# Decay arguments of the state space groups: made by TensorE and ScalarE from on-chip rows instead of loaded by DMA

## The chip, the cores and the metric

The kernel runs on one core of one Trainium2 chip. The metric is the device time of one execution in microseconds (us), as the median of some runs. All times below are for that one core.

## The reference, cut to what matters

The kernel computes two transformer-like blocks over 512 tokens of width 1024. The change touches the first block's state space branch: 32 heads in 8 groups of 4 (R = 4), each run forwards and backwards over 4 chunks of 128 tokens.

```
xbc = silu(depthwise_conv(xbc, conv_w, conv_b))        # 5 taps
a_cs   = cumsum(dt * a)                                # per head, within a chunk
decay  = exp(where(mask, a_cs[l] - a_cs[s], -inf))     # 128 x 128 per head, chunk, direction
cb     = einsum('bclgn,bcsgn->bcgls', c, b)
y_diag = einsum('bcgls,bcgrls,bcsgrp->bclgrp', cb, decay, xdt)
states = einsum('bclgn,bcgrl,bclgrp->bcgrpn', b, decay_states, xdt)
y_off  = einsum('bclgn,bcgrpn,bcgrl->bclgrp', c, prev, exp(a_cs))
y = y_diag + y_off + xs * d_skip;  y = y * silu(z)     # then a norm per group
```

The argument of the decay is the difference of two entries of the same cumulative sum. For each head one of them runs along the 512 tokens in a row, the other is a number per partition.

## The kernel before, in words

**Weights.** All large matrix products stream their weights. SyncE loads `raw` in quarters (`load_quarter`, L240), ScalarE rounds it to `w_hi` (`make_hi`, L248), GpSimd makes the remainder `w_lo` (`make_lo`, L255), and TensorE runs three products for each (`main_step`, L279). One step is 12 matmuls of 512 columns; a panel is 8 steps. A `w_hi` can be written only when the step that used that place, a panel earlier, is done.

**A group.** Under 12 such steps TensorE does a group's small products (`ssd_pe`, L1550): states after step 2 (two) and step 4 (one), the four heads' `pe_y` after steps 3, 4, 5 and 6, the products with the earlier states `pe_off` 0 after step 6 and 1 and 2 after step 7, and for the next group the transposes and the c by b product `pe_turn` (0, 1 after step 9; 2, 3 after step 11). Four PSUM banks `main` hold the panels. Four more, `aux0` to `aux3`, hold the small products: `aux0` and `aux1` the result y of all four heads, `aux2` and `aux3` everything else in turn. The semaphores `aux_free` say how often `aux2` and `aux3` have been emptied. `pe_off(2)` writes `aux3`, so it waits for VectorE to have emptied `pe_off(0)` from it (`take_off(0)`).

**Decay.** `cs_dram` holds the rows of the cumulative sum. ScalarE's queue loads for each head both directions' rows, spread over all partitions, into `dmat[r]` (`load_decay`, L582: 512 KB). VectorE subtracts the per-partition number twice (L1800), takes the smaller of both directions into `e_buf` (L1801), ScalarE exponentiates (L1232), and VectorE multiplies with `cb_m` (`weigh`, L1805).

**VectorE's order in a group** (`ssd_group`, L1790): `xdt` (L1846), decay 0 and 1, weigh 0 and 1, decay 2 and 3, states 0 and 1 (L1813 to L1819), weigh 2 and 3, states 2, first pair of the next group's convolution (L1760 the centre tap, L1769 the four others), `take_off` 0 to 2 (L1830, L1840), second pair of the convolution, y from `aux0` and `aux1` (L1869), the gate (L1872), `mask_cb` (L1779). GpSimd does `xw` (L1079, two of 1024 columns) and the skip term (L1083) at a group's start and otherwise `w_lo`. ScalarE does `w_hi`, the Silus (L1193), the copies out of the banks (`take_x`, L1187, twice per pair of groups; `take_turned`, L1198 and L1202), and the squares (L1274). The order on each engine is written out by hand; seven cycles lead from group 0 to group 7, and groups 0 to 5 run in a loop of pairs (`half` 0 and 1).

**Before group 0**, ScalarE's queue also stores 4 MB of attention bias rows (`rel_rows`, L1180).

Of the kernel before, what the change touches and what calls it, by code (L numbers as in the profile page):

```python
# [24 lines left out]
P = 128  # L25
# [66 lines left out]
def two_blocks(nc, d, out):  # L92
    ctx = ExitStack()
    with ctx:
# [44 lines left out]
        cst_sb = at("cst_sb", B0 + 60 * KB, [64, TOK])  # L139
# [19 lines left out]
        e_buf = [at("e_buf0", R0 + 32 * KB, [P, TOK]), at("e_buf1", R0 + 34 * KB, [P, TOK])]  # L159
# [65 lines left out]
        cs_dram = nc.dram_tensor("cs_rows", (2, G, R, TOK), F32, kind="Internal").ap()  # L225
# [117 lines left out]
        cs_stored, rel_stored = sem("cs_stored"), sem("rel_stored")  # L343
# [228 lines left out]
        decay_landed = [sem(f"decay_landed{h}") for h in range(R)]  # L572
        xdt_done, xw_done, skip_done = sem("xdt_done"), sem("xw_done"), sem("skip_done")
        arg_done, decay_done, t_done = sem("arg_done"), sem("decay_done"), sem("t_done")
        states_full = sem("states_full")
# [5 lines left out]

        def load_decay(eng, g, r):  # L582

            if isinstance(g, int):
                src = bass.AP(cs_dram.tensor, (g * R + r) * TOK, [[0, P], [NH * TOK, 2], [1, TOK]])
            else:
                row = cs_dram[:, bass.ds(g, 1), r, :]
                src = bass.AP(row.tensor, row.offset, [[0, P], [NH * TOK, 2], [1, TOK]])
            eng.dma_start(dmat[r][:, :, :], src).then_inc(decay_landed[r], 16)

# [19 lines left out]
        def pe_turn(eng, g, part):  # L610
# [14 lines left out]
        def pe_states(eng, g, i):  # L625
# [8 lines left out]
        def pe_y(eng, g, r):  # L634
# [8 lines left out]
        def pe_off(eng, g, i):  # L643
# [485 lines left out]
        def _(act):  # L1129
# [47 lines left out]
            act.wait_ge(dt_dve, 4)  # L1177
            act.dma_start(cs_dram.rearrange("a g r t -> (a g r) t"), cst_sb[:, :]).then_inc(cs_stored, 16)
# [5 lines left out]
            def take_x(p):  # L1184
                for m in range(4):
                    wait_full(act, p, p, m)
                    act.activation(u_raw[:, m, :], mb[m][:, :], ACT.Copy).then_inc(bank_free, 1)  # L1187

# [23 lines left out]
            take_turned(0, 0)  # L1212
            hi(2, range(6, 7))
# [3 lines left out]
            hi(2, [7])  # L1217

            def ssd_act(gp, half):
# [10 lines left out]
                def decay_exp(r):  # L1230
                    act.wait_ge(arg_done, g * 4 + r + 1)
                    act.activation(e_buf[r % 2][:, :], e_buf[r % 2][:, :], ACT.Exp).then_inc(decay_done, 1)  # L1232

                decay_exp(0)
                decay_exp(1)
                slots(0, 4 - half)
# [6 lines left out]
                decay_exp(2)  # L1243
                decay_exp(3)
                slots(4, 7)
                if not last:
                    for r in range(R):
                        act.wait_ge(y_full, g * 4 + (r + 1))
                        load_decay(act, g + 1, r)
# [5 lines left out]
                if not last:  # L1255
# [3 lines left out]
                    slots(8, 9)  # L1259
# [23 lines left out]

# [177 lines left out]
        def _(pe):  # L1461
# [74 lines left out]
            def turn_first(k):  # L1536
# [7 lines left out]
                if k == 5:  # L1544
                    pe_turn(pe, 0, 2)
                if k == 6:
                    pe_turn(pe, 0, 3)
# [631 lines left out]
```

## Time and profile before

| | us |
|---|---|
| median of 3 runs | 2009.14 (2003.4, 2009.14, 2009.41) |
| the profiled execution | 2006.3 |
| its span | 2004.5 |
| first `xdt` of group 0 | 103.79 |
| first `xdt` of group 7 | 515.85 |

The profile is one execution of the program. Its span is 1.8 us shorter than that execution's time. Times in its rows count from the span's start. Durations of neighbouring VectorE, ScalarE and TensorE rows overlap by some hundredths to tenths of a microsecond, since one instruction drains while the next starts; the pace is the distance of the starts.

### The profile page before, as it was taken

To read this page: it belongs to the slowest core of one execution; us is meant where nothing else is said; L and a number is where in the kernel's file an instruction comes from. 1 tells how busy PE (TensorE), PEld (TensorE's weight loads), DVE (VectorE), ACT (ScalarE), POOL (GpSimd) and SP (SyncE) were. 2 spreads that over 40 slices of the span, in tenths; PEclk is the share of its full clock that TensorE was granted. 3 is DMA by queue.
4 is the path that set the end of the run, shared out by engine and by line. 5 is a ranking of instruction groups with operands and counts; after the bars stand their busy time and mean duration, and the time that the engine had idled before them with its cause. 6 is when DMAs were issued, how large, how long until landed. Compare 5 with 4: busy or idle time off the path is not lost.

```text
span 2004.5 us, 27105 instructions
## 1 busy us (share of the span) xinstructions
PE 1838.4 (92%) x8948; PEld 1518.2 (76%) x8948; DVE 964.1 (48%) x1306; ACT 793.2 (40%) x1627; POOL 841.3 (42%) x598
## 2 busy tenths in 40 slices
PE   5698898898789999998999999999989999999988
PEld 4577677777668787877888888877878888787766
DVE  4389898999931456423432022132072112445754
ACT  4233333334232465532443234334343332466542
POOL 4244443445734312243554444454474444441312
PEclk9898998999889999999999999999999999999989
DMA  4742223233112312142323333333323223221111
GB/s 156 138 139 63 91 84 105 94 94 88 60 45 93 111 43 89 47 132 74 94 90 100 95 95 95 102 97 126 94 74 95 84 84 99 80 79 52 63 32 53
DMA packets 55011, 176.76 MB, mean 88 GB/s; under 512 B 5291, under 2 KB 7723, under 8 KB 54668
## 3 DMA queue, kind: packets, MB, share of 16 engines
q1 hardware_dynamic: 38592, 140.53, 22.9%
q10 hardware_dynamic: 16332, 35.11, 6.5%
q8 instruction: 50, 0.82, 0.2%
q14 instruction: 37, 0.30, 0.1%
HBM read 169.19 MB, written 6.42 MB: 88 GB/s over the span
## 4 chain that ended last, share of the span: by engine, by line
PE 62%; DVE 18%; issue 12%; POOL 4%; ACT 3%; DMA 1%; DVEq 1%; ACTq 0%; POOLq 0%
PE main L294 46%; DVE dmat L1800 5%; PE aux L773 3%; PE main L322 3%; POOL w_lo L257 2%; PE main L1604 2%; DMA dmat<-cs_rows 1%; PE aux L638 1%; DVE y_all L1840 1%; PE aux L760 1%; PE aux L747 1%; DVE u_acc L1769 1%; PE aux L364 1%; DVE dmat L1805 1%; DVE off_t L1830 1%
## 5 line engine op out<-in xcount | busy, mean ns | idle before, releaser
L257 POOL TENSOR_TENSOR w_lo<-raw,w_hi 128x512 fp32r<-128x512 f32 x504 | 709.0, 1414 | 1035.9 <-ACT w_hi L253 1021.9
L253 ACT ACTIVATE w_hi<-raw 128x512 fp32r<-128x512 f32 x486 | 301.7, 629 | 697.3 <-PE main L294 684.2
L294 PE MATMUL main<-w_hi,a_hi 128*128 128x512 f32 x752 | 319.1, 424 | 2.3 <-ACT vv L1381 1.4
L294 PE MATMUL main<-w_hi,a_lo 128*128 128x512 f32 x752 | 299.7, 399 | 0.0
L294 PE MATMUL main<-w_lo,a_hi 128*128 128x512 f32 x752 | 299.3, 398 | 0.0
L294 PE MATMUL main<-a_hi,w_hi 128*128 128x512 f32 x576 | 235.9, 410 | 2.2 <-ACT u_raw L1187 2.2
L294 PE MATMUL main<-a_lo,w_hi 128*128 128x512 f32 x576 | 228.5, 397 | 0.0
L294 PE MATMUL main<-a_hi,w_lo 128*128 128x512 f32 x576 | 228.2, 396 | 0.0
L294 PEld LDWEIGHTS main<-w_hi,a_lo 128*128 128x128 f32 x752 | 144.6, 192 | 32.2
L294 PEld LDWEIGHTS main<-w_hi,a_hi 128*128 128x128 f32 x752 | 145.9, 194 | 30.3 <-ACT vv L1381 1.8
L294 PEld LDWEIGHTS main<-w_lo,a_hi 128*128 128x128 f32 x752 | 146.0, 194 | 24.5
L294 PE MATMUL main<-w_hi,f_hi 128*128 128x512 f32 x352 | 139.3, 396 | 1.6 <-DVE f_lo L377 1.6
L294 PE MATMUL main<-w_hi,f_lo 128*128 128x512 f32 x352 | 137.8, 391 | 0.0
L294 PE MATMUL main<-w_lo,f_hi 128*128 128x512 f32 x352 | 137.7, 391 | 0.0
L294 PEld LDWEIGHTS main<-a_hi,w_hi 128*128 128x128 f32 x576 | 111.4, 193 | 26.0 <-issue 3.1
L294 PEld LDWEIGHTS main<-a_hi,w_lo 128*128 128x128 f32 x576 | 110.8, 192 | 24.0
L294 PEld LDWEIGHTS main<-a_lo,w_hi 128*128 128x128 f32 x576 | 111.4, 193 | 22.8
L773 PEld LDWEIGHTS aux<-v_sb,pt 128*128 128x128 f32 x544 | 70.3, 190 | 40.6 <-ACT pt L844 23.2
L1769 DVE SCALAR_TENSOR_TENSOR u_acc<-u_raw,par,u_acc 128x510 f32<-128x510 f32 (+1 forms) x128 | 97.1, 828 | 0.0
L1800 DVE TENSOR_TENSOR dmat<-dmat,cs_sb 128x512 f32<-128x512 f32 x64 | 91.4, 1428 | 4.1 <-DMA dmat<-cs_rows 0.5
L773 PE MATMUL aux<-v_sb,pt 128*128 x544 | 83.6, 279 | 6.2 <-ACT pt L844 3.9
L814 ACT ACTIVATE pr<-lg,small 128x384 f32<-128x384 f32 (+1 forms) x128 | 70.5, 553 | 24.8 <-DVE small L800 24.8
(287 smaller groups left out, 3098.5 us busy)
## 6 DMA issues: line engine op xcount, KB each, us to landing
raw<-w_stream_in SPq DMA_DIRECT2D x264, 512.0 KB, 3.5
dmat<-cs_rows ACTq DMA_DIRECT2D x32, 512.0 KB, 9.4
x_res<-x_in ACTq DMA_DIRECT2D x8, 512.0 KB, 4.8
rel_rows<-rel_row ACTq DMA_DIRECT2D x1, 4096.0 KB, 44.4
bias<-rel_rows ACTq DMA_DIRECT2D x2, 1536.0 KB, 7.7
out<-x_res SPq DMA_DIRECT2D x4, 512.0 KB, 2.6
bgate<-b_gate_in ACTq DMA_DIRECT2D x4, 256.0 KB, 5.5
ln_g<-ln_g_in ACTq DMA_DIRECT2D x1, 1024.0 KB, 6.6
```

The lines of the kernel that those rows point to most:

```text
L253: eng.activation(w_hi[:, k, :], raw[:, k, :], ACT.Copy).then_inc(hi_done, 1)
L257: eng.tensor_tensor(w_lo[:, k, :], raw[:, k, :], w_hi[:, k, :].bitcast(F32), ALU.subtract).then_inc(lo_done, 1)
L294: mm = eng.matmul(mb[m][:, :], lhs, rhs, start=(first and k == 0 and n == 0), stop=(last and k == KT - 1 and n == 2))
L322: mm = eng.matmul(out, lhs, rhs, start=(first and k == 0 and n == 0), stop=(last and k == KT - 1 and n == 2))
L364: t = eng.transpose(b[:, m * P:m * P + P], self.src[:, m, c:c + P], ident)
L638: x = eng.matmul(ab[c // 2][:, (c % 2) * GW + r * HP:(c % 2) * GW + r * HP + HP], dmat[r][:, dr, c * P:c * P + P], xdt[:, dr, c, r * HP:r ...
L747: eng.matmul(ab[c % 2][:, 0:nb * P], q, self.k_hh[half][:, keys], start=True, stop=False)
L773: x = eng.matmul(ab[3][:, c * HP:c * HP + HP], pt[c % 2][:, b * P:b * P + P], v_sb[:, lo + b, bass.ds(j * P + half * HP, HP)], start=(b == ...
L814: eng.activation(pr[t % 2][:, c, 0:self.w], lg[t % 2][:, c, 0:self.w], ACT.Exp, bias=small[:, ng + c:ng + c + 1], accum_out=small[:, sm + ...
L1604: mm = pe.matmul(mb[m][:, :], lhs, rhs, start=False, stop=(k == KT - 1 and n == 2))
L1769: ins = dve.scalar_tensor_tensor(acc, u_raw[:, m, i0:i0 + o1_ - o0], tap(m, k), acc, ALU.mult, ALU.add)
L1800: ch(dve.tensor_tensor(dm[:, dr], dm[:, dr], cs, ALU.subtract))
```

## The change

Nothing is loaded for the decay any more. The rows of the cumulative sum stay on chip, rounded part in the upper and remainder in the lower 64 partitions of `cs_hl`; `pick` and `picked` hold ones that choose a head's two rows.

- TensorE: `pe_arg` (two matmuls of 512 columns per head) writes a head's row, spread over all partitions, to `aux0` (one direction) and `aux1` (the other). Head 0 runs after step 8 and waits for `y_taken` (VectorE has taken the last group's y from both banks); heads 1, 2 and 3 run after steps 9, 10 and 11, each behind `arg_done` of the head before.
- ScalarE: `take_arg` copies `aux0` with the per-partition number added, in four pieces of 128 columns, into the head's own half tile `dmat[r][:, 1]`. The exponential works there in place. `centre` does the convolution's centre tap and bias (four instructions per group). Four DMA issues per group go.
- VectorE: `arg_min` adds the number to `aux1` and takes the minimum with the tile, in four pieces of 128 columns. The 8 subtractions of L1800, 4 minima of L1801 and 4 centre taps of L1760 per group go.
- Order on VectorE: states 2 stands behind the convolution's first pair, y is taken right after the second pair, and all of `take_off` comes behind y. Weigh 0, 1 and 2 stand ahead of the states.

```diff
-        def load_decay(eng, g, r):
...
+        def pe_arg(eng, g, r, half):
+
+            if r == 0:
+                eng.wait_ge(pick_set, g + 1)
+                if not (isinstance(g, int) and g == 0):
+                    eng.wait_ge(y_taken, g)
+            else:
+                eng.wait_ge(arg_done, g * 4 + r)
+            for dr in range(2):
+                one_row = picked[:, half, dr, r:r + 1].broadcast_to((P, P))
+                x = eng.matmul(ab[dr][:, :], one_row, cs_hl[:, :], start=True, stop=True)
+            x.then_inc(arg_full, 1)
...
+            def centre(g, taken, pair):
...
+                    act.activation(u_acc[:, m, :], u_raw[:, m, :], ACT.Identity, bias=par[:, bass.ds(g * 4 + (PC["conv_b"] + m), 1)],
+                                   scale=par[:, bass.ds(g * 20 + (PC["conv_w"] + m * 5 + 2), 1)]).then_inc(centred, 1)
+
+            def take_arg(g, r):
+
+                act.wait_ge(arg_full, g * 4 + (r + 1))
+                if not (isinstance(g, int) and g == 0):
+                    act.wait_ge(y_full, g * 4 + (r - 3))
+                for c in range(NT):
+                    cs = slice(c * P, c * P + P)
+                    x = act.activation(dmat[r][:, 1, cs], ab[0][:, cs], ACT.Identity, bias=cs_sb[:, c, bass.ds(g * R + r, 1)])
+                x.then_inc(arg_in, 1)
...
             take_x(0)
+            act.wait_ge(dt_dve, 4)
+            pick_rows(0, 0)
+            centre(0, 0, 0)
+            centre(0, 0, 1)
             hi(2, range(0, 3))
-            for n in range(4):
-                silu(0, n)
-            hi(2, range(3, 6))
-            act.wait_ge(cs_stored, 16)
-            for r in range(R):
-                load_decay(act, 0, r)
+            act.wait_ge(dt_dve, 6)
+            take_arg(0, 0)
+            silu(0, 0)
+            silu(0, 1)
...
                     silu(g + 1, 2)
                     silu(g + 1, 3)
+                    slots(8, 9)
+                    take_arg(g + 1, 0)
                     slots(9, 10)
                     take_turned(g + 1, 0)
+                    take_arg(g + 1, 1)
                     slots(10, 11)
                     if half == 1:
                         take_x(gp * 3 + (P_Z + 2))
+                    take_arg(g + 1, 2)
+                    decay_exp(g + 1, 0)
                     slots(11, 12)
                     take_turned(g + 1, 2)
                     take_turned(g + 1, 3)
+                    take_arg(g + 1, 3)
+                    decay_exp(g + 1, 1)
+                    decay_exp(g + 1, 2)
...
+            def arg_min(g, r):
+
+                dve.wait_ge(arg_in, g * 4 + (r + 1))
+                for c in range(NT):
+                    e = dmat[r][:, 1, c * P:c * P + P]
+                    x = dve.scalar_tensor_tensor(e, ab[1][:, c * P:c * P + P], cs_sb[:, c, bass.ds(g * R + (NH + r), 1)], e,
+                                                 ALU.add, ALU.min)
+                x.then_inc(arg_done, 1)
+
             conv(0, 0, 0)
+            arg_min(0, 0)
             conv(0, 0, 1)
+            arg_min(0, 1)
             mask_cb(0)
+            arg_min(0, 2)
...
-                decay(0)
-                decay(1)
+                arg_min(g, 3)
                 weigh(0)
                 weigh(1)
-                decay(2)
-                decay(3)
+                weigh(2)
                 take_states(0)
                 take_states(1)
-                weigh(2)
                 weigh(3)
-                take_states(2)
                 if not last:
                     conv(g + 1, gp * 12 + (4, 12)[half], 0)
-                for i in range(3):
-                    take_off(i)
+                take_states(2)
                 if not last:
                     conv(g + 1, gp * 12 + (4, 12)[half], 1)
...
+                dve.wait_ge(y_taken, g + 1)
+                for i in range(3):
+                    take_off(i)
+                if not last:
+                    arg_min(g + 1, 0)
```

What stands in a row on VectorE behind the convolution's first pair of group 1, before (`off_t<-aux3` is `take_off(0)`, which frees `aux3`):

```order
L1769 ISA [waits dve_chain]
L1769 SCALAR_TENSOR_TENSOR u_acc_98<-u_raw_97,par_56,u_acc_98 128x510
L1830 REGISTER_ALU [waits off_full]
L1830 TENSOR_TENSOR off_t_101<-aux3,e_cs_59 128x256
L72 REGISTER_ALU
L1830 ISA [waits dve_chain]
```

And behind the second pair of the same group, in the changed kernel:

```order
L1827 SCALAR_TENSOR_TENSOR u_acc_100<-u_raw_99,par_56,u_acc_100 128x510
L1926 ISA [waits skip_done,y_full]
L1926 TENSOR_TENSOR y_all_85<-y_all_85,aux0 128x2x256
L72 REGISTER_ALU
L1926 ISA [waits dve_chain]
L1926 TENSOR_TENSOR y_all_85<-y_all_85,aux1 128x2x256
L1891 REGISTER_ALU [waits off_full,y_taken]
L1891 TENSOR_TENSOR off_t_101<-aux3,e_cs_59 128x256
L72 REGISTER_ALU
L1891 ISA [waits dve_chain]
L1891 TENSOR_TENSOR off_t_101<-aux3,e_cs_59 128x256
```

`take_off(0)` has moved from between the two pairs to behind both of them and behind the two additions of y.

On TensorE, the small products after step 7 of group 0 in the changed kernel (as before, the third waits for `aux3`):

```order
L658 MATMUL aux2<-hst_97,c_st_88 128x256 [waits aux2_free]
L658 MATMUL aux2<-hst_97,c_st_88 128x256
L658 MATMUL aux3<-hst_97,c_st_88 128x256 [waits aux3_free]
L658 MATMUL aux3<-hst_97,c_st_88 128x256
L282 REGISTER_ALU
```

And after step 9 of the same group, before:

```order
L622 MATMUL aux2<-const_55,u_acc_98 128x128 [waits silu_done]
L622 MATMUL aux2<-const_55,u_acc_98 128x128 x3
L615 REGISTER_ALU [waits aux3_free]
L620 MATMUL aux3<-c_st_86,u_acc_98 128x128 [waits silu_done]
L620 MATMUL aux3<-c_st_86,u_acc_98 128x128 x3
L282 REGISTER_ALU
```

and in the changed kernel, with the argument of head 1 behind them:

```order
L626 MATMUL aux2<-const_55,u_acc_100 128x128 [waits silu_done]
L626 MATMUL aux2<-const_55,u_acc_100 128x128 x3
L619 REGISTER_ALU [waits aux3_free]
L624 MATMUL aux3<-c_st_88,u_acc_100 128x128 [waits silu_done]
L624 MATMUL aux3<-c_st_88,u_acc_100 128x128 x3
L611 MATMUL aux0<-cs_hl_77,picked_79 128x512 [waits arg_done]
L611 MATMUL aux1<-cs_hl_77,picked_79 128x512
```

TensorE gains two matmuls of 512 columns there, and with them a wait for VectorE's minimum of the head before.

## Rows read from the trace of the kernel before

**Rows 1.** Windows by cycle: length, busy PE PEld DVE ACT POOL, PEclk, DMA, GB/s.
```profile
282.90:343.00 60.10, 53.65 (x256) 45.00 (x256) 52.38 (x61) 22.49 (x46) 26.20 (x15) 0.90 0.33 91
458.90:515.80 56.90, 51.26 (x254) 43.13 (x254) 54.70 (x61) 19.57 (x38) 26.38 (x15) 0.95 0.33 93
```

**Rows 2.** Timeline, TensorE, group 3: start, us, instruction, [idle before it <-releaser].
```profile
305.56 2.07 PE L631 MATMUL aux<-xw,b_tok 128*128 128x256 f32 x4 [3.48 <-DVE hst L1813]
339.82 1.11 PE L622 MATMUL aux<-const,u_acc 128*128 128x128 f32 x4 [2.63 <-DVE cb_m L1779]
```

**Rows 3.** Chain of waits in order of time, group 3: start, us, work.
```profile
307.63 4.62 PE main L294 x12
313.98 2.81 PE main L294 x12
316.79 1.73 PE aux L638 x16
318.52 0.92 PE aux L652 x4
```

**Rows 4.** Timeline of VectorE in group 3.
```profile
282.88 2.36 DVE L1846 TENSOR_TENSOR xdt<-x_tok,dt_sb 128x1024 f32<-128x1024 f32 x2 [2.08 <-ACT x_tok L1202]
319.72 0.98 DVE L1830 TENSOR_TENSOR off_t<-aux,e_cs 128x256 f32<-128x256 f32 x2
329.38 5.37 DVE L1769 SCALAR_TENSOR_TENSOR u_acc<-u_raw,par,u_acc 128x510 f32<-128x510 f32 x8
334.67 1.40 DVE L1869 TENSOR_TENSOR y_all<-y_all,aux 128x512 f32 x2
```

**Rows 5.** Groups by line, VectorE, 282.8 to 343.0: busy, mean ns, idle before.
```profile
L1800 DVE TENSOR_TENSOR dmat<-dmat,cs_sb 128x512 f32<-128x512 f32 x8 | 11.7, 1465 | 0.6
L1801 DVE TENSOR_TENSOR e_buf<-dmat 128x512 f32<-128x512 f32 x4 | 5.3, 1324 | 0.1
L1760 DVE TENSOR_SCALAR u_acc<-u_raw,par 128x512 f32<-128x512 f32 x4 | 2.7, 721 | 0.6 <-DVE hst L1819 0.4 <-DVE y_all L1840 0.3
```

**Rows 6.** Timeline of GpSimd in group 3.
```profile
284.28 5.03 POOL L1079 TENSOR_TENSOR xw<-xdt,e_st 128x1024 f32<-128x1024 f32 x2 [2.46 <-DVE xdt L1846]
295.60 7.19 POOL L257 TENSOR_TENSOR w_lo<-raw,w_hi 128x512 fp32r<-128x512 f32 x4 [3.98 <-ACT w_hi L253]
```

**Rows 7.** One line's instructions each, whole span: duration ns min/median/max.
```profile
L1817 DVE TENSOR_TENSOR hst<-hst,dec x16: 676/692/2375, 128.0 to 543.7; 128x512 f32<-128x512 f32 x16
...
L1819 DVE TENSOR_TENSOR hst<-hst,aux x16: 686/686/689, 128.7 to 546.1; 128x512 f32<-128x512 f32 x16
...
L1830 DVE TENSOR_TENSOR off_t<-aux,e_cs x48: 409/424/426, 142.0 to 556.1; 128x256 f32<-128x256 f32 x48
```

**Rows 8.** Timeline of ScalarE in group 3.
```profile
285.05 1.28 ACT L1232 ACT_TABLE_LOAD   x1
336.83 2.05 ACT L1187 ACTIVATE u_raw<-main 128x512 f32<-128x512 f32 x4
339.26 0.62 ACT L1202 ACTIVATE x_tok<-aux 128x512 f32<-128x512 f32 x1
```

**Rows 9.** Timeline before group 0: ScalarE's queue, TensorE, VectorE.
```profile
81.93 14.53 ACTq L589 DMA_DIRECT2D dmat<-cs_rows  x4
...
97.16 1.11 PE L622 MATMUL aux<-const,u_acc 128*128 128x128 f32 x4 [15.27 <-ACT b_tok L1198]
...
103.79 2.40 DVE L1846 TENSOR_TENSOR xdt<-x_tok,dt_sb 128x1024 f32<-128x1024 f32 x2 [23.20 <-ACT x_tok L1202]
```

**Rows 10.** Weight loads of SyncE, 40 to 130 us, issue to landing.
```profile
DMA to landing us min/median/max: 3.5/3.6/18.4
```

**Rows 11.** Timeline of the last group: VectorE, GpSimd.
```profile
515.85 2.36 DVE L1846 TENSOR_TENSOR xdt<-x_tok,dt_sb 128x1024 f32<-128x1024 f32 x2 [0.38 <-ACT x_tok L1202]
558.95 1.22 DVE L1872 TENSOR_TENSOR y_all<-y_all,sz 128x1024 f32<-128x1024 f32 x1
...
540.26 13.27 POOL L603 TENSOR_TENSOR y_all<-y_all,ssq 128x1024 f32<-128x1024 f32 x6
```

More of the change, by code:

```diff
@@ L606, in y_group, with pe_turn @@
             return y_all[:, :, bass.ds(g * GW, GW)]
-        def pe_turn(eng, g, part):
+        def pe_arg(eng, g, r, half):
[9 more added lines that the diff above has]
+            x.then_inc(arg_full, 1)
+        def pe_turn(eng, g, part, half):
             bank = part % 2
@@ L623, in pe_turn, with pe_states @@
             x.then_inc(turned, 1)
-        def pe_states(eng, g, i):
+        def pe_states(eng, g, i, half):
             if i == 0:
@@ L632, in pe_states, with pe_y @@
             x.then_inc(states_full, 1)
-        def pe_y(eng, g, r):
+        def pe_y(eng, g, r, half):
+            if r == 0:
+                eng.wait_ge(arg_done, g * 4 + 4)
             eng.wait_ge(t_done, g * 4 + r + 1)
@@ L641, in pe_y, with pe_off @@
             x.then_inc(y_full, 1)
-        def pe_off(eng, g, i):
+        def pe_off(eng, g, i, half):
             bank = (i + 1) % 2
@@ L1187, in take_x, with decay_exp, pick_rows @@
                     act.activation(u_raw[:, m, :], mb[m][:, :], ACT.Copy).then_inc(bank_free, 1)
+            def centre(g, taken, pair):
+                two = TILES[2 * pair:2 * pair + 2]
+                act.wait_ge(bank_free, taken + (max(two) + 1))
+                for m in two:
+                    act.activation(u_acc[:, m, :], u_raw[:, m, :], ACT.Identity, bias=par[:, bass.ds(g * 4 + (PC["conv_b"] + m), 1)],
[8 more added lines that the diff above has]
+                x.then_inc(arg_in, 1)
+            def decay_exp(g, r):
+                act.wait_ge(arg_done, g * 4 + (r + 1))
+                act.activation(dmat[r][:, 1, :], dmat[r][:, 1, :], ACT.Exp).then_inc(decay_done, 1)
+            def pick_rows(g, half):
+                act.activation(picked[:, half], pick[:, :].rearrange("p (a h) -> p a h", a=2)[:, :, bass.ds(g * R, R)], ACT.Copy).then_inc(pick_set, 1)
             def silu(g, n):
@@ L1217, in _ @@
             hi(2, [7])
+            take_arg(0, 3)
+            for r in range(3):
+                decay_exp(0, r)
             def ssd_act(gp, half):
@@ L1228, in slots @@
                         make_hi(act, gp * 3 + (P_Z + 1 + q // 8), q % 8)
[L1230 to L1236, printed above, removed]
+                slots(0, 1)
+                decay_exp(g, 3)
+                if not last:
+                    pick_rows(g + 1, 1 - half)
+                slots(1, 4 - half)
                 if half == 1:
@@ L1242, in ssd_act @@
                     slots(3, 4)
-                decay_exp(2)
-                decay_exp(3)
-                slots(4, 7)
+                taken = gp * 12 + (4, 12)[half]
                 if not last:
-                    for r in range(R):
-                        act.wait_ge(y_full, g * 4 + (r + 1))
-                        load_decay(act, g + 1, r)
+                    centre(g + 1, taken, 0)
+                slots(4, 5)
+                if not last:
+                    centre(g + 1, taken, 1)
+                slots(5, 7)
                 if half == 0:
@@ L1281, in _ @@
             ssd_act(3, 1)
+            act.wait_ge(rel_stored, 16)
             op_y.act(act, [0, 1])
@@ L1758, in conv @@
                 dve.wait_ge(bank_free, taken + (max(two) + 1))
-                for m in two:
-                    ch.count(dve.tensor_scalar(u_acc[:, m, :], u_raw[:, m, :], tap(m, 2), par[:, bass.ds(g * 4 + (PC["conv_b"] + m), 1)],
-                                               ALU.mult, ALU.add))
+                dve.wait_ge(centred, g * 4 + (2 * pair + 2))
                 for k in (0, 1, 3, 4):
@@ L1867, in ssd_group @@
                         dve.wait_ge(y_full, g * 4 + 4)
+                        dve.wait_ge(skip_done, g + 1)
                     y2 = y_group(g)[:, 2 * t2:2 * t2 + 2, :]
-                    ch(dve.tensor_tensor(y2, y2, ab[t2][:, :].rearrange("p (c n) -> p c n", c=2), ALU.add))
+                    ins = dve.tensor_tensor(y2, y2, ab[t2][:, :].rearrange("p (c n) -> p c n", c=2), ALU.add)
+                    if t2:
+                        ins.then_inc(y_taken, 1)
+                    else:
+                        ch(ins)
+                dve.wait_ge(y_taken, g + 1)
+                for i in range(3):
+                    take_off(i)
+                if not last:
+                    arg_min(g + 1, 0)
                 dve.wait_ge(bank_free, gp * 12 + (4 * O_Z + 4))
@@ L1873, in ssd_group @@
                 if not last:
+                    arg_min(g + 1, 1)
                     mask_cb(g + 1)
-            per = len(TILES) * 4 + 1 + 2 * R + 2 + 3 + 6 + 2
+                    arg_min(g + 1, 2)
+            per = len(TILES) * 3 + 1 + 2 + 3 + 6 + 1
             with dve.Fori(0, 3) as gp:
```

70 lines of the change are left out of this document (36 added, 34 removed).

## The prediction

> **What bounds the kernel now.** I read three views, in this order. First the windows by group: a cycle, from one group's `xdt` to the next's, takes 57 to 60 us, TensorE is busy for 51 to 54 of them and VectorE for 52 to 55 [rows 1]. From 103.79 [rows 9] to 515.85 [rows 11] seven cycles take 412.1 us, 58.9 each. Then TensorE's timeline of group 3: it idles twice, 3.48 us for VectorE's state copy and 2.63 us for `mask_cb` [rows 2], both times because VectorE is late. Then the chain: behind such an idle a step takes 4.62 us, an undisturbed one 2.81 [rows 3]; the granted clock of a cycle is 0.90 to 0.95 [rows 1], so of 60.1 us some 12, of 56.9 some 6 ran at 1.2 instead of 2.4 GHz: 6 and 3 us of work lost for two idles, 1.5 to 3 for each. So VectorE sets the pace, through TensorE's waits and the clock after them. Before group 0, TensorE idles 15.27 us while ScalarE's queue issues four decay loads behind the 4 MB store (14.53 us) [rows 9].
>
> **The change part by part.** I follow one cycle, with T the start of `xdt` and group 3 as the model.
>
> Removed from VectorE: 8 L1800 and 4 L1801, 11.7 + 5.3 = 17.0 us, and 4 L1760, 2.7 us [rows 5]. Twelve instructions of about 0.69 us (the L1817 median, [rows 7]) would be 8.3, so 8.7 of the 17.0 is waiting. It falls where GpSimd works: `xw` and four `w_lo` run side by side with them [rows 6]. That GpSimd work stays, and what now stands beside it is `weigh` and the convolution, which read two SBUF tiles as L1800 did. The rows split by operand: L1817 (two SBUF inputs) goes from 676 to 2375 ns, L1819 and L1830 (one input from PSUM) stay within 686 to 689 and 409 to 426 [rows 7]. So I carry all 8.7 over to the new neighbours; the lower bound is 0. The Trainium skill (SBUF — State Buffer, "Who interferes with whom") says the same as a lock: of a VectorE instruction with two SBUF inputs and a GpSimd one that reads SBUF, the second to start blocks for the other's whole length. By that rule none of the 8.7 is saved; without it all of it would be.
>
> Added to VectorE: 16 pieces of `arg_min` with one PSUM input. 256 columns take 0.42 us [rows 7], 512 about 0.69, so 128 about 0.29: 1.15 us per head, 4.6 per group, of which head 3's stands behind `xdt` and three heads' at the end. Bounds 0.8 (pace without overlap of drains) and 2.8 per head (as 512-column instructions). Centre taps, ScalarE: 4 of about 0.62 us (as `x_tok`, [rows 8]); ScalarE idles long at those places, its bound is the same from above, nothing from below, and I take 0.
>
> The point that decides: **`take_off(0)` moves behind both convolution pairs and y**, and `pe_off(2)`, on TensorE after step 7, waits for it to empty `aux3`. Queued behind `pe_off(2)` are steps 8 to 11 and all arguments and transposes of the next group. VectorE's time from T to the end of `take_off(0)`'s products: before, T to the end of the second pair is 329.38 + 5.37 - 282.88 = 51.9 [rows 4]. Minus 17.0; minus 329.38 - 319.72 = 9.7 (all of `take_off` and two L1760) [rows 4]; minus the other two L1760, 1.3: 23.9. Plus 1.15 for head 3, plus 8.7 carried over, plus 1.4 for y and 1.0 for the products [rows 4], plus 1.3 for one `w_lo` more beside the second pair (295.60: 7.19 for four, 1.8 each with VectorE beside it) [rows 6]: **37.4 us**. Bounds: 27.4 (nothing carried over, no extra `w_lo`) and 40.
>
> TensorE reaches `pe_off(2)` 8 x 2.81 + four `pe_y` of 1.73 + four small products of about 0.9 [rows 3] = 33.0 us after its step 0 starts, and that start lies 0.3 to 1.9 us ahead of T. So it idles about 5 to 6 us there, where it now idles 3.5 and 2.6 elsewhere. Cost in clock: 1.5 to 3 us per idle from above; I take 2.3 once.
>
> From there TensorE leads: `pe_off(2)` 0.92, four steps 11.2, three arguments 3 x 2 x 0.23 = 1.4 (a step's 2.81 / 12 per matmul) [rows 3], two small products 1.1 (one of them at low clock took 1.11 [rows 2]): 14.6 to the end of step 11. The arguments' hand-overs (ScalarE 0.8, VectorE 1.15) are hidden by a step of 2.81 as long as ScalarE is free. Then, in the first group of a pair: transposes 1.1, `x_tok` 0.62 [rows 8], signals 0.3: 2.0. In the second, ScalarE does `take_x` ahead of `take_arg(2)`: copies after step 11 0.7 (the last of four in 2.05), `take_arg(2)` 0.8, table load 1.28 and exponential 0.63, a `w_hi` 0.5, two `x_tok` 1.1, signals 0.3 [rows 8]: 5.3. So the cycles are 37.4 + 14.6 + 2.3 + 2.0 = 56.3 and 59.6 us. Seven: 4 x 56.3 + 3 x 59.6 = 404.0 against 412.1: **-8 us**. The decay's shorter chain is nearly eaten by the later `take_off(0)`.
>
> Start: the 15.27 idle goes. New there: `take_x` behind three more small instructions (about 1.7), VectorE's second pair behind head 0's argument (which waits for TensorE's step 3), TensorE's head 2 behind that pair, and head 3's argument behind `take_x(1)`: I take 6 of them on the path. Net **-9**, bounds 0 and -15.3. The 4 MB store stays; it is needed only by the attention.
>
> Last group: before, 515.85 to the gate's end 560.2, 44.3 us [rows 11]. The 17.0 are gone there too, but `take_off` comes last, and GpSimd's six norms (13.27 [rows 11]), which read SBUF, then run beside its additions and the gate. I take **-5**, bounds 0 and -12.
>
> Sum: 2006.3 - 8 - 9 - 5 = 1984. The profiled execution (2006.3) is 2.8 below the median of the runs (2009.1), so I put **1987**.
>
> **The rivals.**
> - A, the waiting goes with the instructions: VectorE needs 33 us or less to `take_off(0)`, TensorE no longer idles, and a cycle is TensorE's work: 60.1 - 3.5 - 2.6 - 6 = 48 plus four arguments 1.9, 50, and 53 in second groups. Seven: 359, -53; with start and end 1942. Against: [rows 7] and [rows 6]. Chance 0.1. Half way (34 to 36 us and a shorter low clock), about 1965: 0.15.
> - B, slower: the arguments' round trips. TensorE may not start the next head before ScalarE and VectorE have finished the last. After 5 to 6 us idle step 8 runs at 1.2 GHz; if VectorE, with `take_off`, the gate and `w_lo` beside it, is later than TensorE at heads 1, 2 and 3, TensorE idles again after each step and stays at 1.2 GHz for more of the 14.6 us. Half of it more at that level is 4 us a cycle, 28 in all: 2015. It decides from 4 us a cycle on. For: 2.6 us idle already brings the low level [rows 2, 3]; against: the slack per head is a whole step. Chance 0.15.
> - C, the start gives nothing: the 4 MB store holds back the weight loads (18.4 us to landing against 3.6 [rows 10]), and an earlier group 0 waits for weights instead: 1996. Chance 0.12.
> - The forecast itself, 1975 to 2003: 0.48.
>
> **How the numbers follow.** About 0.3%, 6 us, is what a measurement of this kernel can tell from no change. The forecast gives 0.43 faster and 0.05 same or slower; A 0.25 faster; C 0.06 faster, 0.05 same, 0.01 slower; B 0.14 slower, 0.01 same: faster 0.74, same 0.10, slower 0.16. The range takes in the half-way case and B at its price, and leaves out A in full: 1948 to 2017.
>
> **What would show it.** In the profile after: TensorE idle 5 to 6 us before the third small product after step 7, released by VectorE's `off_t`, in all groups; hardly any idle before the states or the transposes. `weigh` (1024 columns, as `xdt`, of which two take 2.36 [rows 4]) well above 1.2 us for the first two of a group. `arg_min` pieces within 0.25 to 0.35 us whatever GpSimd does. Second groups some 3 us longer than first ones. First `xdt` near 92, with weigh 0 near 98. If the idle before `pe_off(2)` is under 2 us, A holds; if the idles stand before the arguments, B. I would be wrong altogether if VectorE got to `take_off(0)` as late as 40 us after T.

## The result and the profile after

The changed kernel takes **1952.19 us** (median of 4 runs, 1950.18 to 1952.57) against 2008.74 (median of 4, 2003.4 to 2009.41) for the kernel before: a ratio of 0.9722, 95% interval 0.9704 to 0.974. That is 56.5 us less, where 22 were forecast. The direction and the places were as forecast, the size was not.

The profiled execution has a span of 1948.4 us, 56.1 less than the 2004.5 of before. The starts of `xdt` divide it into three parts; they answer to the `xdt` rows of [rows 4, 9, 11]. Timeline of VectorE, changed kernel (start, us, instruction, idle before and its releaser):

```profile
95.14 2.40 DVE L1907 TENSOR_TENSOR xdt<-x_tok,dt_sb 128x1024 f32<-128x1024 f32 x2 [3.30 <-ACT x_tok L1235]
...
254.02 2.43 DVE L1907 TENSOR_TENSOR xdt<-x_tok,dt_sb 128x1024 f32<-128x1024 f32 x2 [2.36 <-ACT x_tok L1235]
308.34 2.40 DVE L1907 TENSOR_TENSOR xdt<-x_tok,dt_sb 128x1024 f32<-128x1024 f32 x2 [2.37 <-ACT x_tok L1235]
...
464.27 2.51 DVE L1907 TENSOR_TENSOR xdt<-x_tok,dt_sb 128x1024 f32<-128x1024 f32 x2 [2.29 <-ACT x_tok L1235]
```

| part | before | after | measured | forecast |
|---|---|---|---|---|
| to the first `xdt` | 103.79 | 95.14 | -8.7 | -9 |
| seven cycles | 412.06 | 369.13 | -42.9 | -8 |
| from the eighth `xdt` on | 1488.6 | 1484.1 | -4.5 | -5 |

All that the forecast missed lies in the seven cycles: a cycle leads from one group's `xdt` to the next's, and `first` and `second` groups are the two of a pair in the loop. Windows by cycle, group 2 and group 3, in the columns of [rows 1]:

```profile
202.85:254.02 51.17, 50.74 (x263) 42.91 (x262) 45.18 (x60) 27.42 (x60) 27.14 (x16) 0.99 0.20 61
254.02:308.34 54.32, 50.97 (x261) 42.53 (x260) 43.91 (x60) 29.62 (x64) 29.09 (x16) 0.98 0.19 58
```

TensorE is now busy for 50.7 of 51.2 us in first groups of a pair and for 51.0 of 54.3 in second ones. In [rows 1] it was busy for 53.7 of 60.1, with a granted clock of 0.90. Within the cycles it still waits for two things, by its waits from 107 to 505 us (us in total, times, longest):

```profile
PE aux L611 <- DVE dmat L1849: 6.3, 3, 2.1
PE aux L658 <- DVE off_t L1891: 5.5, 7, 1.2
```

The two idles of [rows 2] are gone. In their place stand one of 1.2 us before `pe_off(2)` (L658), where 5 to 6 us were forecast, and in second groups alone one of 2.1 us before head 3's argument (L611). Here are both in TensorE's timeline of group 3:

```profile
285.71 1.02 PE L658 MATMUL aux<-hst,c_st 128*128 128x256 f32 x4
287.97 1.13 PE L658 MATMUL aux<-hst,c_st 128*128 128x256 f32 x4 [1.24 <-DVE off_t L1891]
...
302.88 1.03 PE L626 MATMUL aux<-const,u_acc 128*128 128x128 f32 x8
306.02 0.84 PE L611 MATMUL aux<-cs_hl,picked 128*128 128x512 f32 x2 [2.11 <-DVE dmat L1849]
```

VectorE's timeline of the same group shows the stretch that the forecast put at 37.4 us, from `xdt` to the end of `take_off(0)`'s products. It runs from 254.02 to 287.91, 33.9 us, and every group between the first and the last but one takes 33.8 or 33.9:

```profile
257.40 7.57 DVE L1866 TENSOR_TENSOR dmat<-cb_m,dmat 128x1024 f32<-128x1024 f32 x3
264.89 0.68 DVE L1874 COPY hst<-aux 128x512 f32<-128x512 f32 x1
265.78 0.89 DVE L1878 TENSOR_TENSOR hst<-hst,dec 128x512 f32<-128x512 f32 x1 [0.21 <-DVE hst L1874]
266.70 0.69 DVE L1880 TENSOR_TENSOR hst<-hst,aux 128x512 f32<-128x512 f32 x1
267.43 1.47 DVE L1866 TENSOR_TENSOR dmat<-cb_m,dmat 128x1024 f32<-128x1024 f32 x1
268.82 8.45 DVE L1827 SCALAR_TENSOR_TENSOR u_acc<-u_raw,par,u_acc 128x510 f32<-128x510 f32 x8
...
278.98 6.39 DVE L1827 SCALAR_TENSOR_TENSOR u_acc<-u_raw,par,u_acc 128x510 f32<-128x510 f32 x8 [0.39 <-DVE hst L1880]
...
286.92 0.99 DVE L1891 TENSOR_TENSOR off_t<-aux,e_cs 128x256 f32<-128x256 f32 x2
```

And GpSimd beside it; it answers to [rows 6]:

```profile
255.49 5.56 POOL L1085 TENSOR_TENSOR xw<-xdt,e_st 128x1024 f32<-128x1024 f32 x2 [1.26 <-DVE xdt L1907]
261.02 2.87 POOL L1089 TENSOR_TENSOR y_all<-x_tok,par 128x1024 f32 x1
263.85 9.55 POOL L257 TENSOR_TENSOR w_lo<-raw,w_hi 128x512 fp32r<-128x512 f32 x5
276.64 2.39 POOL L257 TENSOR_TENSOR w_lo<-raw,w_hi 128x512 fp32r<-128x512 f32 x1 [3.23 <-ACT w_hi L253]
```

`weigh` took over the neighbours of the removed instructions, as forecast: three take 7.57 us beside `xw` and the skip product. In VectorE's timeline of the kernel before two took 2.35:

```profile
294.25 2.35 DVE L1805 TENSOR_TENSOR dmat<-cb_m,e_buf 128x1024 f32<-128x1024 f32 x2
```

But the whole stretch is 3.5 us shorter than forecast, and that decided whether TensorE idles for long.

### The profile page after: what moved, and what is told of

Same layout as the page of the kernel before. It is cut to its first block, busy times and chain, and to the rows that moved or that the text cites. A ratio compares the mean times of both kernels' runs of the same rounds, so it can differ in the third digit from the quotient of the medians.

```text
span 1948.4 us, 27496 instructions
## 1 busy us (share of the span) xinstructions
PE 1832.3 (94%) x9012; PEld 1515.9 (78%) x9012; DVE 902.1 (46%) x1308; ACT 856.6 (44%) x1796; POOL 853.6 (44%) x598
## 4 chain that ended last, share of the span: by engine, by line
PE 61%; issue 19%; DVE 8%; POOL 6%; ACT 2%; DVEq 0%; DMA 0%; POOLq 0%; ACTq 0%
PE main L294 49%; POOL w_lo L257 5%; PE aux L779 2%; PE main L322 2%; DVE u_acc L1827 2%; PE aux L611 1%; PE main L1661 1%; PE aux L635 1%; PE aux L1738 1%; PE aux L766 1%; PE aux L364 1%; PE aux L644 1%; DVE vv L2051 1%; DVE x_res L555 1%; PE aux L753 1%
## 5 line engine op out<-in xcount | busy, mean ns | idle before, releaser
L294 PE MATMUL main<-a_hi,w_hi 128*128 128x512 f32 x576 | 230.9, 401 | 3.2 <-ACT u_raw L1193 3.2
L1827 DVE SCALAR_TENSOR_TENSOR u_acc<-u_raw,par,u_acc 128x510 f32<-128x510 f32 (+1 forms) x128 | 118.0, 992 | 7.7 <-issue 4.7
L294 PEld LDWEIGHTS main<-w_hi,f_hi 128*128 128x128 f32 x352 | 66.7, 189 | 15.3 <-DVE f_lo L377 2.0
```

Of the source, the lines that this page charges most:

```text
L294: mm = eng.matmul(mb[m][:, :], lhs, rhs, start=(first and k == 0 and n == 0), stop=(last and k == KT - 1 and n == 2))
L1827: ins = dve.scalar_tensor_tensor(acc, u_raw[:, m, i0:i0 + o1_ - o0], tap(m, k), acc, ALU.mult, ALU.add)
```

## The experiments

Times are of one run each where no range is given. The kernel before, run again beside these, had medians of 2005.39 us and 2006.47 (7 runs each) and, in one single run, 2004.59. Cycles and waits are always those of one profiled execution. "The stretch" is always `xdt` to the end of `take_off(0)`'s products, and "low clock" the time within the seven cycles in which the record of TensorE's granted clock shows 1.2 instead of 2.4 GHz. The changed kernel has a stretch of 33.9 us, 10.2 us of low clock in all, and 369.1 us for the seven cycles; the kernel before had 54.6 and 412.1.

**Is the place of `take_off(0)` the price of the change?** First, the kernel before with only that move: all three of `take_off` behind both pairs and y.

```
-                for i in range(3):
-                    take_off(i)
                 if not last:
                     conv(g + 1, gp * 12 + (4, 12)[half], 1)
...
+                for i in range(3):
+                    take_off(i)
```

> The kernel before with one part of the change alone: take_off 0 to 2 behind the convolution's second pair and y. Theory 1: take_off(0) then comes 51.9 - 8.0 + 1.4 + 1.0 = 46 us after xdt, plus TensorE's 13.2, clock loss 2.5 and 2.0: cycles of 63 to 65 us against 58.9, 30 to 40 us slower in all, about 2043. Theory 2: the same work in another order, 2009 within 5.

Measured: 2043.31 us, seven cycles of 62.9 to 65.0 us, 446 in all. TensorE waits:

```profile
PE aux L652 <- DVE off_t L1830: 42.1, 6, 8.3
PE aux L631 <- DVE hst L1813: 17.8, 6, 3.5
```

By the time the move alone costs 37.9 us, by the cycles 34.0. So the step on which the forecast rested, `pe_off(2)` waiting for `take_off(0)`, exists; the change moves it and pays for it with the instructions that it removes.

Then the changed kernel with `take_off(0)` back between the pairs:

```
                 take_states(2)
+                take_off(0)
                 if not last:
                     conv(g + 1, gp * 12 + (4, 12)[half], 1)
...
-                for i in range(3):
+                for i in range(1, 3):
                     take_off(i)
```

> The changed kernel with take_off(0) put back between states 2 and the convolution's second pair; the rest as changed. Theory 1 (a cycle is TensorE's own work, 50 us and 53 in second groups, unless VectorE reaches take_off(0) later than about 33 us after xdt starts; each us later costs a us, and 2 to 3 more once TensorE has idled long enough to lose its clock): TensorE's wait of about 1 us before pe_off(2) goes in all 8 groups, 6 to 9 us in all, about 1945. Theory 2 (the place of take_off does not matter, the gain is VectorE's lighter load alone): 1952, no change.

Measured: 1976.93 us (4 runs, 1974.95 to 1978.47; ratio 0.9854, 0.9837 to 0.987), 25 slower than the changed kernel where 7 less were expected. Two rows tell why, VectorE's timeline of group 3 and TensorE's waits:

```profile
295.13 0.99 DVE L1891 TENSOR_TENSOR off_t<-aux,e_cs 128x256 f32<-128x256 f32 x2 [4.72 <-PE aux L658]
...
PE aux L611 <- DVE y_all L1927: 23.2, 7, 3.5
```

VectorE is now so early that it stands 4.72 us for TensorE's `pe_off(0)`. The second pair and y are queued behind that wait, so y comes late, and head 0's argument, which needs y's banks empty, comes up to 3.5 us late in each of the seven cycles, 23.2 in all. So this old place is right for the old VectorE and wrong for the new one. The expectation had looked at the bank that becomes free and not at what stands behind the wait.

**How steep is the stretch?** The changed kernel with instructions added on VectorE directly ahead of y, one or three clearings of 1024 columns.

```
                     conv(g + 1, gp * 12 + (4, 12)[half], 1)
+                for _ in range(3):
+                    ch(dve.memset(pad_t[:, :], 0.0))
                 for t2 in range(2):
```

> The changed kernel with three memsets of 1024 columns (some 3.3 us) on VectorE ahead of taking y, in each group. Theory 1: take_off(0) comes 37.3 us after xdt, where the prediction had put it, and the cycles become its 56.3 and 59.6 us: seven of them 35 us longer, about 1988, with 1.2 GHz back in each group behind the wait before pe_off(2). If the clock stays up: 23 us longer, 1975. Theory 2: VectorE idles 6 to 9 us per cycle, so 3.3 us more are absorbed: at most 1957.

> The changed kernel with one memset of 1024 columns (1.2 us, a third of what three cost) on VectorE ahead of y. Theory 1: take_off(0) at 35.1 us after xdt, each cycle 1.2 us longer as long as the clock stays up: 1961; up to 1968 if the longer wait already costs clock. Rival (clock loss alone makes the difference between 34 and 37.6 us): under 3 us, 1954.

Measured: three give 1986.76 us, one gives 1956.39. TensorE's waits with three, then with one:

```profile
PE aux L659 <- DVE off_t L1892: 32.1, 7, 4.9
```

```profile
PE aux L659 <- DVE off_t L1892: 15.2, 8, 2.5
```

| variant | stretch | longest idle before `pe_off(2)` | low clock | seven cycles |
|---|---|---|---|---|
| changed kernel | 33.9 | 1.2 | 10.2 | 369.1 |
| one clearing | 35.2 | 2.5 | 10.2 | 380.0 |
| three clearings | 37.6 | 4.9 | 41.0 | 410.3 |

One clearing lengthens stretch and cycles alike: +1.3 us, +1.3 to +1.4 in six of the seven cycles. With three, the stretch is 3.7 us longer, 26 us in seven cycles, and 30.8 us more run at half the clock, which is 15 us of work lost: 41, and 41.1 are measured. This is the forecast's own formula checked at the forecast's own stretch: at 37.6 us first groups take 55.8 to 58.7 us and second ones 60.3 to 60.8, against 56.3 and 59.6 in the prediction. That the padded kernel's time is the forecast 1987 to the microsecond is partly luck: its seven cycles are 6 us longer than the forecast's 404, and what follows them is 3 us shorter, and the forecast has 2.8 us on top for the step from the profiled execution to the median. (One clearing moved the single run by only 4.2 us from the changed kernel's median, though its cycles are 10.9 longer. By the two profiled executions it is 6.2, and the part behind the eighth `xdt` is 4.2 shorter, see below.)

**What is the centre tap on ScalarE worth?** The changed kernel with the four taps back on VectorE.

```
-                dve.wait_ge(centred, g * 4 + (2 * pair + 2))
+                for m in two:
+                    ch.count(dve.tensor_scalar(u_acc[:, m, :], u_raw[:, m, :], tap(m, 2), ...
```

> The changed kernel, with the four centre taps and biases of a group on VectorE again. They lie ahead of take_off(0), 4 x 0.68 = 2.7 us. T1 (VectorE's stretch sets the cycle one for one, as one padding instruction showed, and above about 2 us of idle the 1.2 GHz spell is added): the stretch 36.6 us, cycles 3 to 4 us longer, about 1974. Rival (the centre tap's move is worth nothing, since VectorE had slack): 1952.

Measured: 1968.24 us, 16 slower; the stretch 35.5 to 36.5, TensorE's wait for `off_t` 3.9 us at the longest, cycles 54.4 and 58.5, low clock 27.3 us. The seven cycles are 22 us longer, as the slope of the two padded kernels would have it: about 14 from the stretch, 9 from the clock. So a part of the change that removes 2.7 us a group brings 16 us by the single run and 22 by the cycles.

**Where does VectorE's waiting come from, and how much of it did the change do away with?** The forecast took it from instruction lengths. These two kernels measure it: GpSimd keeps its instructions in the groups, but each touches only a few columns (weights' low halves 16 of 512, `xw` and skip product 2 of a head's 64), so parts of the result are left out.

```
-                    make_lo(pool, p, k)
+                    pool.tensor_tensor(w_lo[:, k, 0:16], raw[:, k, 0:16], w_hi[:, k, 0:16].bitcast(F32),
+                                       ALU.subtract).then_inc(lo_done, 1)
```

> The kernel before, with the same cut of GpSimd's work in the seven cycles (the same parts left out). T1: from xdt to the end of the second convolution pair VectorE took 51.9 us, of which about 11 were waiting; it should take about 41, the eight subtractions that read two SBUF tiles fall from 11.7 to about 6 us, and the stretch shortens by about 11 here but by only about 6 in the changed kernel: the difference, 4 to 5 us, is the waiting that the change did away with and that the prediction carried over. T2 (all waiting was tied to the removed instructions or to none): the two shortenings are equal within 1 us.

> The changed kernel, with GpSimd's work in the seven cycles cut to a few columns (w_lo 16 of 512 columns, xw and the skip product 2 of 32 columns of a head, after one clearing of both tiles in group 0; so part of xw, y and the weights' low halves is left out). T1 (what VectorE lost in the 33.9 us from xdt to the end of take_off(0)'s products was waiting for GpSimd): weigh falls from 1.9 to 2.9 us to about 1.25 each, the stretch to about 27.5 us (33.9 - 6.3), in groups after the first; TensorE then never waits for off_t, cycles stay near 50 and 53 us, since TensorE is the bound there. T2 (weigh is long by its own operands, not by GpSimd): the stretch stays within 1 us of 33.9.

Measured: the kernel before 1941.52 us, the changed one 1942.32. Busy time of VectorE (the third after the length) in group 3, from `xdt` to the end of the second pair, in the kernel before and in it with small GpSimd work:

```profile
282.88:334.75 51.87, 48.39 (x238) 41.02 (x237) 47.56 (x56) 15.66 (x30) 21.46 (x12) 0.92 0.33 91
```

```profile
261.59:305.15 43.56, 43.56 (x233) 37.52 (x232) 36.09 (x56) 16.05 (x30) 6.62 (x12) 1.00 0.34 107
```

and the stretch in the changed kernel and in it with small GpSimd work:

```profile
254.02:287.91 33.89, 32.71 (x177) 27.82 (x175) 32.77 (x35) 15.69 (x34) 23.42 (x12) 1.00 0.20 62
```

```profile
257.57:288.35 30.78, 30.78 (x170) 26.74 (x169) 24.37 (x35) 13.71 (x31) 5.20 (x10) 1.00 0.23 68
```

The same instructions lose 47.56 - 36.09 = **11.5 us** to GpSimd before, and 32.77 - 24.37 = **8.4 us** after. The forecast had left 2.3 beside instructions that stay, carried 8.7 over and added 1.3: about 12.3. `weigh` and the old subtractions, by line (busy, mean ns), from the changed and from the old kernel with small GpSimd work:

```profile
L1876 DVE TENSOR_TENSOR dmat<-cb_m,dmat 128x1024 f32<-128x1024 f32 x24 | 28.2, 1217 | 0.2
```

```profile
L1810 DVE TENSOR_TENSOR dmat<-dmat,cs_sb 128x512 f32<-128x512 f32 x48 | 33.6, 700 | 2.9
L1811 DVE TENSOR_TENSOR e_buf<-dmat 128x512 f32<-128x512 f32 x24 | 16.6, 692 | 0.8
```

In a group that is, by the kernel before with small GpSimd work, 5.6 + 2.8 = 8.4 us for the twelve removed instructions instead of 17.0 [rows 5], so 8.6 were waiting; 8.7 were forecast. All of `weigh`'s excess is GpSimd too: its 1217 ns here stand against up to 2.9 us beside `xw`.

Where the 8.4 are can be read by laying the same rows of the changed kernel with small GpSimd work beside those of VectorE's timeline of group 3 above:

```profile
260.88 3.49 DVE L1876 TENSOR_TENSOR dmat<-cb_m,dmat 128x1024 f32<-128x1024 f32 x3
268.15 1.23 DVE L1876 TENSOR_TENSOR dmat<-cb_m,dmat 128x1024 f32<-128x1024 f32 x1
272.03 5.38 DVE L1837 SCALAR_TENSOR_TENSOR u_acc<-u_raw,par,u_acc 128x510 f32<-128x510 f32 x8 [2.65 <-ACT u_acc L1210]
279.12 5.38 DVE L1837 SCALAR_TENSOR_TENSOR u_acc<-u_raw,par,u_acc 128x510 f32<-128x510 f32 x8 [0.39 <-DVE hst L1890]
```

`weigh` loses 7.57 - 3.49 = 4.1 us in its row of three and 0.2 in the fourth, the first pair of the convolution 8.45 - 5.38 = 3.1, the second 6.39 - 5.38 = 1.0, one state product 0.2. (By rows this adds up to 0.2 more than the busy times, since rows overlap.)

Two expectations fell in part. The old kernel's stretch to the end of the second pair is 43.6 us without GpSimd and not about 41, and the two kernels' waiting differs by 3.1 and not 4 to 5. And the changed kernel's stretch is 30.8 us and not 27.5: the waiting went, but VectorE then stands for others, 2.65 us for ScalarE's centre tap ahead of the first pair, 1.4 for the states, 1.2 for y in group 3. It has overtaken TensorE. Cycles by windows, the changed kernel, then the kernel before, each with small GpSimd work:

```profile
206.93:257.57 50.64, 50.64 (x260) 42.97 (x260) 34.41 (x60) 27.44 (x60) 6.14 (x15) 0.97 0.21 62
257.57:310.19 52.62, 50.51 (x262) 42.57 (x261) 34.42 (x60) 29.51 (x64) 6.38 (x15) 0.99 0.20 60
```

```profile
312.02:360.15 48.13, 46.64 (x249) 39.97 (x248) 39.91 (x61) 18.99 (x35) 7.35 (x15) 1.00 0.36 110
```

This comparison says most about who was on the path. Its first cycle has to be left out, since in both of these kernels GpSimd clears nine tiles there, about 9 us in a row, before its `xw`, and TensorE waits for that; here in the changed kernel with small GpSimd work, in its waits from 95 to 154 us:

```profile
PE aux L635 <- POOL xw L1085: 3.7, 1, 3.7
```

In the six cycles behind it the **old** kernel needs 294 us without GpSimd in its way, the changed one 309: it gives TensorE four arguments more a group, about 1.8 us at 0.23 a matmul (an estimate), and has 10 us of low clock where the old one has none. GpSimd costs the old kernel 57 us in these six cycles and the changed one 7: the old one's VectorE was on the path, the changed one's hardly is.

**The start.** The kernel before without the decay loads; VectorE's subtraction reads other numbers, so the result is not the decay.

```
-            for r in range(R):
-                load_decay(act, 0, r)
...
-                        ch(dve.tensor_tensor(dm[:, dr], dm[:, dr], cs, ALU.subtract))
+                        ch(dve.tensor_tensor(dm[:, dr], cbm[:, dr], cs, ALU.add))
```

> The kernel before without the decay loads (32 transfers of 512 KB); VectorE's L1800 adds the numbers to cb_m instead, so that the decay is not the reference's, with the same instructions and sizes. It measures the part of the change that the transfers and their issue make. Theory 1: only the start gains, 9 to 13 us (the 15.3 us idle ahead of the turn), cycles stay at 58.9: about 1997. Theory 2 (transfers slow the group's cycles too): cycles 1 to 2 us shorter, 1985.

Measured: 1988.36 us, between the two theories and nearer to the second. The first `xdt` starts at 88.11, 15.7 us earlier: just the 15.27 of idle in [rows 9], and more than the 9 to 13 expected. The change got 8.7 of it, so what it adds at the start costs 7.0 (forecast: 6). The seven cycles are 6.0 us shorter, 0.9 each by one profile, from 2.7 shorter to 0.5 longer. So of the 42.9 us that the change gains there, the loads themselves account for some 6 by this profile; the forecast had put them at nothing.

**Better versions.** Second groups are 3.1 us longer, because ScalarE does four `take_x` copies, head 2's argument and a table load in a row. Timeline of ScalarE in group 3, changed kernel:

```profile
301.02 2.65 ACT L1193 ACTIVATE u_raw<-main 128x512 f32<-128x512 f32 x4 [0.72 <-PE main L294]
303.57 1.13 ACT L1210 ACTIVATE dmat<-aux,cs_sb 128x128 f32<-128x128 f32 x4
304.72 1.28 ACT L1216 ACT_TABLE_LOAD   x1
```

One edit puts `take_arg(2)` ahead of `take_x`, and the first exponential behind head 3's argument; a second puts `take_off(0)` directly ahead of y; then both.

```
                     slots(10, 11)
+                    take_arg(g + 1, 2)
                     if half == 1:
                         take_x(gp * 3 + (P_Z + 2))
-                    take_arg(g + 1, 2)
-                    decay_exp(g + 1, 0)
```

> The changed kernel with ScalarE's take_arg(2) ahead of take_x in second groups, and the exponential of head 0 behind take_arg(3). Theory 1: the 3.1 us by which second groups are longer are TensorE and VectorE waiting for ScalarE's copies, argument, table load and exponential ahead of x_tok; 2.5 to 3 us less in each of three groups, about 1944. Rival (first groups are paced by something else of the same size behind it): less than 3 us, 1950.

> The changed kernel with take_off(0) directly ahead of taking y, behind the convolution's second pair. Put between the pairs it had made VectorE wait for TensorE's pe_off(0), and y_taken late. Theory 1 (VectorE's time to take_off(0) against TensorE's arrival at pe_off(2), and then y_taken against its arrival at pe_arg(0)): take_off(0) ends 1.6 us earlier, at 32.3 us after xdt, TensorE's wait there (about 1 us each) goes, y_taken has some 3 us of slack: 7 to 9 us faster, 1944. Rival (y_taken decides as it did in the run with take_off(0) between the pairs): no gain or slower, 1952 to 1960.

> Both of these edits. Theory 1: the gains add, since they stand at two places of the cycle: about 1936, all cycles near 50 us, TensorE's own work. Rival (one wait hides the other): 1942 to 1944.

| variant | us (4 runs each) | ratio to before (95%) | seven cycles |
|---|---|---|---|
| `take_arg(2)` first | 1938.90 (1938.44 to 1941.12) | 0.9664 (0.9645 to 0.9683) | 358.8 |
| `take_off(0)` before y | 1947.78 (1945.91 to 1948.86) | 0.9702 (0.9683 to 0.9721) | 370.6 |
| both | 1936.12 (1935.78 to 1937.86) | 0.9649 (0.9631 to 0.9668) | 359.3 |

The first takes the 2.1 us idle out of second groups: they take 51.3 us, nearly as the first ones (50.8), and the clock never falls in the seven cycles. The second shortens the stretch to 32.2 us and first groups' cycles from 51.2 to 49.7, but second groups' grow from 54.3 to 56.7. TensorE's timeline of a second group there shows a new idle before head 1's argument, with the old one before head 3's behind it:

```profile
191.86 0.84 PE L611 MATMUL aux<-cs_hl,picked 128*128 128x512 f32 x2 [1.99 <-DVE dmat L1849]
203.13 0.73 PE L611 MATMUL aux<-cs_hl,picked 128*128 128x512 f32 x2 [2.12 <-DVE dmat L1849]
```

TensorE no longer waits at `pe_off(2)`, reaches head 1 sooner, and there VectorE is still busy with `take_off`. That is rival B's mechanism, at 2 us. The kernel with both edits is the fastest of all, 0.8% below the changed one. But its seven cycles are no shorter than with the first edit alone (first groups 49.3, second ones 52.5 to 54.0): in the cycles the gains do not add, and the 2.8 us between the two medians are less than the 0.3% that a measurement can tell apart.

## Why the prediction was wrong in size

- **The path: right.** VectorE set the pace before, and the place that decides after is `pe_off(2)` against `take_off(0)`; moving that alone costs the old kernel 38 us.
- **VectorE's own work: right.** The rest of 23.9 us and the additions hold; pieces of `arg_min` take 0.28 us each in a row of four (0.29 forecast), 0.34 each by itself.
- **The failing step is the term "carry all 8.7 over" in the 37.4 us.** The stretch is 33.9. The amount tied to the removed instructions was right (8.6 measured); that it all comes back beside the new neighbours was not. Of waiting for GpSimd the stretch has 8.4 us, where the sum implied about 12.3. By the rows of group 3, `weigh` now loses 4.3 us where it lost 0.2, the first pair 3.1 where it lost 2.1 (7.44 us in the row below, 5.37 without GpSimd), and a state product 0.2: so 4.1 + 1.0 + 0.2 = 5.3 came back and not 8.7. The extra 1.3 at the second pair was right in the main (1.0).

```profile
312.36 7.44 DVE L1769 SCALAR_TENSOR_TENSOR u_acc<-u_raw,par,u_acc 128x510 f32<-128x510 f32 x8
```

- **Why only part came back** is a reading of these rows and was not tested by itself. Two of the five `w_lo` in a row from 263.85 now meet the state copy and the addition, which read PSUM and keep their 0.68 and 0.69 us. And the one issued at 276.64 is itself held up, to 2.39 us, while the VectorE instructions beside it keep their length. The neighbours have to be laid out instruction by instruction; the total can't be carried.
- **The clock term, 2.3 us a cycle, fell with it.** It hangs on the idle, and the idle was 1.2 and not 5 to 6 us. The padded kernels show both sides: at 2.5 us of idle no low clock is added, at 4.9 it is. TensorE reaches `pe_off(2)` 32.7 us after `xdt`, at the late end of what the forecast had, so even its 37.4 would have meant 4.7 us of idle. Behind `take_off(0)`, a first group takes 17.3 us to the next `xdt` (forecast 16.6 plus 2.3), a second one 20.4 (19.9 plus 2.3). So of the 5.1 us that a first group's cycle is below the forecast, 3.5 are the stretch and 1.6 the clock; with about the same in second groups, seven times that are the missing 35.
- **Second groups 3 us longer: right** (3.1), for the reason given; with `take_arg(2)` ahead of `take_x` the difference is 0.5.
- **The start: right** in sum (-8.7 against -9), though by 15.7 less 7.0 and not 15.3 less 6. The dates given for it, 92 and 98, were 3 us too early: 95.14 and 100.99. They did not fit the sum's own -9.
- **The last group gave more than -5.** From its `xdt` to the gate's end it takes 35.5 us instead of 44.3 [rows 11]: -8.8. The profiled run of the changed kernel loses 4 of that later, in stages that no edit touches: from the eighth `xdt` to the end it takes 1484.1 us, the variants with GpSimd's full work 1479 to 1482 but for one at 1484, and in the 500 us behind that `xdt` it has 37.5 us of low clock where most of them have 30.7. This is one way in which a variant's time can move by 4 us less or more than its cycles, and the likely reason why the edit with `take_off(0)` before y gains 4.4 us without a gain in the cycles. What sets it was not looked into.
- **The rivals.** By its conditions the half-way case (34 to 36 us, a shorter low clock, about 1965, 0.15) was the nearest; by its time A (TensorE's work alone, 50 and 53 a cycle, 1942) was. TensorE's floor, with GpSimd out of the way, is 50.6 and 52.6 a cycle, and 51.2 and 54.3 are measured. A's condition was not met: it asked for 33 us, and 8.4 us of waiting are still there. They just hardly reach the path any more. Most of the clock's cost lies between 34 and 37.4 us, and the forecast put 0.48 on one side of it on the strength of one term whose own bounds were 0 and 8.7. Of B, one wait stands in the changed kernel, the 2.1 us before head 3's argument in second groups, and another turns up as soon as TensorE is earlier. C did not happen: the first `xdt` came at 95.14.
- **The rule of the Trainium skill** (SBUF — State Buffer, "Who interferes with whom") was taken by the prediction to mean that none of the 8.7 is saved. The Trainium skill says there that a VectorE instruction with two SBUF inputs contends with a GpSimd one that reads SBUF, and one with at most one SBUF input, outside the 2-port modes, does not; that the later one blocks for the whole instruction it words for the 2-port modes. By this case's runs both halves hold: with GpSimd's work small, all 32 `weigh` take 1208 to 1227 ns, and beside full work 1310 to 2925; the state additions, with one input from PSUM, take 686 to 689 ns in the changed kernel and 686 to 687 in it with small GpSimd work. In the row of meetings here a `weigh` (1.22 alone) and an `xw` (1.91 at its shortest) take about 2.9 us each, near the 3.13 of both one after the other. So the rule fits single meetings; the error was in their number, which the prediction took as unchanged.

## What to carry to other kernels

Time lost where two engines meet belongs to the meeting and not to the instruction: count, instruction by instruction, what stands beside the other engine's work after the change, and measure the total by shrinking the other engine's work to a few columns. Where a stretch of one engine races a stretch of another, find out how steep it is on both sides: here 3.7 us more in the stretch cost 5.9 us a cycle, and 1.7 us less brought nothing over seven cycles, since another wait took the place of the one that went. And after moving a release earlier, look at what is queued behind its own wait: it can hold up the next release by more than it gained.

## What the runs showed of the hardware

- The versions with small GpSimd work show GpSimd's full price for a kernel: 57 us in six cycles of the old kernel, 7 in those of the changed one, at hardly different GpSimd work (26.2 and 27 to 29 us busy a cycle).
- TensorE's granted clock: in the changed kernel and with one clearing, with idles of 1.2 to 2.5 us between busy stretches, it stayed at 2.4 GHz nearly throughout (10 us of 369 and of 380 at 1.2 GHz); with 3.9 us 27 of 391, with 4.9 us 41 of 410. The length of the longest idle does not settle it: the kernel before, with one of 3.5 and one of 2.6 in a cycle, had 55 of 412.
- A VectorE instruction of 128 columns with one PSUM input and a column of SBUF as scalar takes 0.34 us by itself, and one follows the other after 0.26.
